# A transformer stack on one core: columns of two input projections reordered, with head norms, index scores and key compression placed between the later panels

## What is computed

```python
def dsa_moba_mixer(h, ...):                                  # block 0, projection "ab_in"
    aq, ak, av, iq, ik, iw, bq, bk, bv = _split(h @ w_in, AB_SIZES)
    aq, ak = partial_rope(rms_norm(aq, ...)), partial_rope(rms_norm(ak, ...))
    iq, ik = partial_rope(iq), partial_rope(ik)              # index heads: no norm
    # score = sum over 8 index heads of iw * relu(iq . ik), causal; the 64 best keys of each query are kept
    o_a = dsa_attention(aq, ak, av, iq, ik, iw)
    bq, bk = partial_rope(rms_norm(bq, ...)), partial_rope(rms_norm(bk, ...))
    o_b = moba_attention(bq, bk, bv)
    return concatenate([o_a, o_b]) @ w_out

def nsa_mixer(h, ...):                                       # block 1, projection "nsa_in"
    q, kc, vc, ks, vs, kw, vw, gt = _split(h @ w_in, C_SIZES)
    q = rms_norm(q, q_norm); q_rot = partial_rope(q)
    kc = rms_norm(nsa_compress(kc, pos_k, w1_k, w2_k), kcmp_norm)   # silu(windows @ w1) @ w2
    vc = nsa_compress(vc, pos_v, w1_v, w2_v)
    ks, kw = partial_rope(rms_norm(ks)), partial_rope(rms_norm(kw))
    gates = sigmoid(gt)
    o = gates . (attention(q, kc, vc), attention(q_rot, ks, vs), attention(q_rot, kw, vw))
    return o @ w_out
```

## Time and profile before

| | us |
|---|---|
| median of 3 runs | 2684.83 |
| the profiled execution's own time | 2688.3 |
| its span | 2686.5 |
| TensorE matmul busy | 2555.4 (95%) |
| VectorE busy | 1120.3 (42%) |
| ScalarE busy | 492.3 (18%) |
| mean granted TensorE clock | 0.959 of full |

### The profile page before, as it was taken

One profiled execution on the slowest core, in us unless ns is written; L12 is line 12 of the kernel. 1 busy time (PEld: TensorE's weight loads), 2 busy tenths in 40 slices (PEclk: granted clock), 3 DMA queues, 4 the chain that ended last, 5 costly groups with the idle time before them and its releaser, 6 DMA issues.

```text
span 2686.5 us, 32881 instructions
## 1 busy us (share of the span) xinstructions
PE 2555.4 (95%) x12508; PEld 2050.3 (76%) x12508; DVE 1120.3 (42%) x2426; ACT 492.3 (18%) x1225; POOL 110.9 (4%) x212
## 2 busy tenths in 40 slices
PE   7789999998898999999999889999999999999997
PEld 4355888846466888588888678889788887689887
DVE  2654212334834023152554445644754553333321
ACT  1132100003512100111210232102123211102210
POOL 0000000000000001000111001110000110000000
PEclk9769999995799999999999999999999999999999
DMA  5113457640023577443777427775326775434441
GB/s 224 65 66 127 150 187 238 226 156 3 1 102 135 181 228 251 147 149 129 256 258 284 147 79 254 258 283 185 117 95 238 258 265 208 166 120 146 150 156 55
DMA packets 122329, 452.98 MB, mean 169 GB/s; under 512 B 13776, under 2 KB 13904, under 8 KB 121680
## 3 DMA queue, kind: packets, MB, share of 16 engines
q1 hardware_dynamic: 92880, 338.24, 35.8%
q0 software_dynamic: 29312, 112.80, 12.2%
HBM read 449.93 MB, written 1.05 MB: 168 GB/s over the span
## 4 chain that ended last, share of the span: by engine, by line
PE 88%; DVE 7%; ACT 2%; issue 1%; DMA 1%; POOL 0%; SPq 0%; DVEq 0%; ACTq 0%
PE pair L460 81%; PE bank L460 6%; DVE att_s L1275 1%; DVE arena L1270 1%; DVE h L1160 1%; ACT arena L941 1%; DVE rstd L1157 1%; PE bank L599 1%; DMA arena<-gmws_dram 1%; ACT arena L953 1%; DVE arena L1678 0%; DVE arena L1674 0%; PE bank L626 0%; DMA cst<-consts_dram 0%; ACT arena L932 0%
## 5 line engine op out<-in xcount | busy, mean ns | idle before, releaser
L460 PE MATMUL pair<-h,ring 128*128 128x256 f32 (+1 forms) x5344 | 1123.6, 373 | 19.6 <-DVE x L1185 6.8
L460 PEld LDWEIGHTS pair<-h,ring 128*128 128x128 f32 x5344 | 989.8, 192 | 149.8 <-DVE x L1185 7.2
L460 PE MATMUL pair<-arena,ring 128*128 128x256 f32 (+1 forms) x3312 | 636.1, 354 | 3.7 <-issue 2.1
L460 PEld LDWEIGHTS pair<-arena,ring 128*128 128x128 f32 x3312 | 567.7, 191 | 72.6 <-issue 3.4
L460 PE MATMUL pair<-ring,h 128*128 128x512 f32 (+1 forms) x768 | 325.5, 584 | 5.5 <-DVE h L1160 3.0
L460 PEld LDWEIGHTS pair<-ring,h 128*128 128x128 f32 x768 | 143.9, 192 | 178.7 <-issue 172.0
L1353 DVE CUSTOM_DVE_ANT_0 adat<-adat,crow,cols 128x1024 f32<-128x1024 f32 x192 | 241.9, 1278 | 8.6 <-DMA adat<-adaw_dram 8.6
L1331 DVE SCALAR_TENSOR_TENSOR arena<-pair,cols,arena 128x255 f32<-128x255 f32 x176 | 84.9, 482 | 279.4 <-ACT arena L989 279.4
L989 ACT ACTIVATE arena<-pair,cols 128x256 f32<-128x256 f32 x176 | 99.2, 564 | 463.3 <-PE pair L460 463.3
L460 PE MATMUL pair<-arena 128*128 128x128 f32 (+7 forms) x946 | 145.0, 359 | 20.6 <-DVE arena L1513 8.6
L911 ACT ACTIVATE h<-x 128x256 f32<-128x256 f32 x84 | 35.0, 417 | 690.4 <-DVE x L1186 364.0
(11 more groups left out here) (197 smaller groups left out, 1310.0 us busy)
## 6 DMA issues: line engine op xcount, KB each, us to landing
ring<-stream_dram SPq DMA_DIRECT2D x638, 512.0 KB, 4.0
adat<-adaw_dram POOLq DMA_DIRECT2D x192, 512.0 KB, 4.6
arena<-gmrows_dram POOLq DMA_DIRECT2D x2, 2560.0 KB, 11.3
arena<-cmpw_dram POOLq DMA_DIRECT2D x1, 2112.0 KB, 8.2
x<-x_in_dram SPq DMA_DIRECT2D x2, 512.0 KB, 4.8
arena<-mem_in_dram SPq DMA_DIRECT2D x1, 1024.0 KB, 12.6
arena<-gmws_dram POOLq DMA_DIRECT2D x2, 512.0 KB, 13.3
out_dram<-h POOLq DMA_DIRECT2D x2, 512.0 KB, 3.8
```

Of the source, the lines that this page charges most:

```text
L460: return nc.tensor.matmul(out, lhsT, rhs, start=start, stop=stop)
```

## The change

The columns of both weight matrices are packed in another order, so that what has most work behind it comes first. For `ab_in`: iq, ik, iw, 88 zero columns, av, k, q, bq, bk, bv. For `nsa_in`: kc, vc, q, ks, kw, vs, vw, gates. The number of tiles stays.

For `ab_in`, in TensorE's program: index transposes behind group 2; index matmuls in four batches of four behind groups 3 to 6, each batch filling two banks with two heads each; the transposes of the other heads in three sets behind groups 5, 7 and 9. ScalarE reads the index banks with ReLU; VectorE's part of the score is then one operation for each head. VectorE's head norms are in three parts (k and q: 9 heads; bq: 8; bk: 8) behind groups 3, 5 and 7, its index rotation behind group 1, and the memory norm moves from group 1 to group 2. For `nsa_in`: transposes of kc and vc behind group 2, the windows behind group 3, compression behind group 4, its output behind group 5, the key norm behind group 6, the transposes of the compressed keys and of q behind group 7, those of the keys behind group 9; the norms of q and the keys in three parts behind groups 3, 5 and 7; the rotation of q behind group 8. The compression writes to banks 5 and 6 instead of 0 and 1. In the diff, TensorE's functions come first, then ScalarE's, then VectorE's with `panels` for `ab_in` and again for `nsa_in`.

```diff
-AB_Q, AB_K, AB_BQ, AB_BK, AB_IQ, AB_IK, AB_AV, AB_BV, AB_IW = 0, 512, 576, 1088, 1600, 1856, 1888, 1952, 2464
-NS_Q, NS_KS, NS_KW, NS_KC, NS_VC, NS_VS, NS_VW, NS_G = 0, 1024, 1280, 1536, 1792, 2048, 2304, 2560
+AB_IQ, AB_IK, AB_IW, AB_AV, AB_K, AB_Q, AB_BQ, AB_BK, AB_BV = 0, 256, 288, 384, 448, 512, 1024, 1536, 2048
+NS_KC, NS_VC, NS_Q, NS_KS, NS_KW, NS_VS, NS_VW, NS_G = 0, 256, 512, 1536, 1792, 2048, 2304, 2560
+AB_PARTS = ((AB_K, 9), (AB_BQ, 8), (AB_BK, 8))
+NS_PARTS = ((NS_Q, 8), (NS_Q + 512, 8), (NS_KS, 8))
...
+                def idx_batch(b):
+                    if b >= 1:
+                        pe.wait_ge(sem("idx_relu"), 2 * b)
+                    for i in range(2):
+                        for a in range(2):
+                            r = 32 * (2 * (b % 2) + a)
+                            last = mm(banks[SB[a]][:, i * TOK:i * TOK + TOK], qrT[r:r + 32, i, b // 2 * P:b // 2 * P + P],
+                                      qrT[r:r + 32, 2, :], True, True)
+                            if i == 1:
+                                last.then_inc(sem("idx_scores"), 1)
+                def ab_between(group):
...
+                    if group == 2:
+                        turns("idx", "idx_rope")
+                    if group == 3:
+                        pe.wait_ge(sem("turn_copied"), turn_sets["idx"][0] + 2)
+                    if 3 <= group < 7:
+                        idx_batch(group - 3)
+                    if group in (5, 7, 9):
+                        turns(f"ab{group // 2 - 2}", "ab_rope", group // 2 - 1)
...
+                def nsa_between(group):
+                    if group == 2:
+                        turns("nsa_c", "freed_dve", FREER[PLAN["nsa_in"].g0 + 1][1])
+                    if group == 4:
+                        compress()
+                    if group == 5:
+                        compress_out()
+                    if group == 7:
+                        pe.wait_ge(sem("kcmp_normed"), 1)
...
+                        turns("nsa_q", "nsa_normed", 2)
+                    if group == 9:
+                        turns("nsa_k", "nsa_rope")
...
                 turn_copies("idx")
-                turn_copies("ab")
+                idx_relu(0)
+                ab_roots(0)
+                idx_relu(1)
+                idx_relu(2)
+                turn_copies("ab0")
+                ab_roots(1)
+                idx_relu(3)
+                turn_copies("ab1")
+                ab_roots(2)
+                turn_copies("ab2")
...
-                roots("nsa_sums", 1, stat[:, 1, 0:TT * 24], P, 1.0 / HD, "nsa_root")
-                act.wait_ge(sem("nsa_gate_in"), 1)
-                nc.scalar.activation(stat[:, 5:7, 0:48], tm[:, :, NS_G:NS_G + 48], ACT.Sigmoid
-                                     ).then_inc(sem("nsa_gates"), 1)
-                turn_copies("nsa_q")
...
                 turn_copies("nsa_c")
-                turn_copies("nsa_k")
+                nsa_roots(0)
                 act.wait_ge(sem("cmp1_done"), 1)
...
                 ins.then_inc(sem("cmp_silu"), 1)
+                nsa_roots(1)
                 roots("kcmp_sums", 1, stat[0:NSA_GROUPS * N_CMP, 2, 0:1], NSA_GROUPS * N_CMP, 1.0 / HD, "kcmp_root")
+                turn_copies("nsa_q")
+                nsa_roots(2)
+                turn_copies("nsa_k")
+                act.wait_ge(sem("nsa_gate_in"), 1)
+                nc.scalar.activation(stat[:, 5:7, 0:48], tm[:, :, NS_G:NS_G + 48], ACT.Sigmoid
+                                     ).then_inc(sem("nsa_gates"), 1)
                 turn_copies("nsa_qr")
...
+                def queries_keys(i):
+                    c0, heads = AB_PARTS[i]
+                    link(heads_normed(i, c0, heads, c0 - AB_K, "ab_sums", "ab_root", i + 1, OT))
+                    rotate(tm[:, :, c0:c0 + heads * HD], heads, HD, 16, 0, view(OT + 1152, 512))
...
+                def index_scores(b):
+                    qt = b // 2
+                    for a in range(2):
+                        dve.wait_ge(sem("idx_relu"), 2 * b + a + 1)
+                        for i in range(2):
+                            hd = 4 * i + 2 * (b % 2) + a
...
+                                ins = V.scalar_tensor_tensor(score[:, qt, :], r, w, score[:, qt, :], ALU.mult, ALU.add)
...
                 def panels(group):
+                    if group == 1:
+                        index_rope()
+                    if group == 2:
+                        memory_norm()
+                    if group == 3:
+                        dve.wait_ge(sem("rows_in"), 16)
+                        queries_keys(0)
+                    if group == 5:
+                        queries_keys(1)
+                        index_scores(0)
+                        index_scores(1)
+                    if group == 7:
+                        queries_keys(2)
+                        V.engine_nop().then_inc(sem("rows_used0"), 1)
+                        index_scores(2)
+                        index_scores(3)
...
                 def panels(group):
+                    if group == 3:
+                        windows()
+                        dve.wait_ge(sem("rows_in"), 16 * 5)
+                        query_parts(0).then_inc(sem("nsa_normed"), 1)
+                    if group == 5:
+                        query_parts(1).then_inc(sem("nsa_normed"), 1)
+                    if group == 6:
+                        compressed()
+                    if group == 7:
+                        link(query_parts(2))
+                        V.engine_nop().then_inc(sem("rows_used2"), 1)
+                        rotated_keys()
+                    if group == 8:
+                        dve.wait_ge(sem("kcmp_turned"), 1)
+                        V.tensor_copy(kcmpT, banks[SB[0]][:, 256:256 + rows]).then_inc(sem("kcmp_done"), 1)
...
+                        rotate(tm[:, :, NS_Q:NS_Q + 1024], NSA_HEADS, HD, 16, 0, view(HID + 4800, 512))
```

## The result

The changed kernel takes **2646.47 us** (median of 4 runs, 2643.95 to 2648.4) against 2686.11 for the kernel before on the same chip (4 runs, 2683.47 to 2687.54): a ratio of 0.9853 [0.9836, 0.987], faster by 39.6 us. Forecast: 2649 (2634 to 2662), 35.9 us gained. The profiled executions span 2643.4 and 2686.5 us.

What follows compares the result with a forecast made beforehand. TensorE, busy 95% of the span, was taken as the bound, with 63 us of gaps behind the two projections to work on. Gains of 21.1 + 13.3 + 1.5 = 35.9 us from a median of 2684.83 gave 2649 us (2634 to 2662).

Steps and rivals of the forecast that it cites:

- ab_in, the sum: From ab_in to the first attention score: score at 104.4 instead of 125.46, 21.1 us gained (19.1 to 21.9).
- Its terms: ab_in's added times: index transposes 0.82 us, four index batches 4.8, head transposes 3.6, last copy to first score 0.7.
- the foreseen wait of 0.62: ab_in's first head transpose set: third job waits 0.6 us for a copy behind two ReLUs on ScalarE.
- nsa_in, the stall and the turns: In nsa_in: 2.58 us stall and 1.9 us of lower clock go; 14 transpose jobs in four sets take 8.8 us.
- The sigmoid of the gates: End of nsa_in: it waits for the last group and adds 0.3 us on ScalarE ahead of the last copies.
- nsa_in, the compression: Behind group 4: clock falls during the step, which takes 10.6 us (6.8 to 13.6); group 5 takes 1.9 us more.
- the forecast's own sign of being wrong: In nsa_in: a compression of 7 or 13.6 us, instead of 10 to 11, would show the forecast wrong.
- Rival 1: In nsa_in: the compression keeps full clock, gaining 5.7 us more, 2643 us in all; chance 0.17.
- Attention 0: First nsa attention: begins at full clock and keeps it for some 3 us, 1.5 us gained.
- Rival 2: nsa attention 0 stays at full clock once it starts there: 11 us, 9.5 beyond those counted, 2639 us; chance 0.12.
- Rivals 3 to 5: Late inserted inputs, 2659 us (0.10); panels lose clock, costing 23 to 110 us (0.02); VectorE's total unchanged, no gain (0.01).
- Total: Whole kernel: 21.1 + 13.3 + 1.5 = 35.9 us gained, giving 2649 us.

Runs made afterwards that it cites:

- e2: Changed kernel with the old ab_in, so only nsa_in has the new column order and inserted work: 2668.67 us, ratio 0.9936 to the kernel before.
- e3: Changed kernel with the 256 compression instructions executed three times in a row behind group 4: 2664.30 us, one execution.
- e4: Changed kernel with the compression issued behind group 3 instead of group 4, so TensorE waits for VectorE's windows directly ahead of it: 2662.07 us, one execution.
- e7: Changed kernel plus four unread matmuls of 256 columns behind the first scores of nsa's attention 0: 2637.47 us, ratio 0.9819 to the kernel before.
- e8: As e7, plus one unread 128-column matmul ahead of each unit's softmax wait in the nsa and DSA attentions: 2633.83 us, ratio 0.9804 to the kernel before.
- e5: Changed kernel with all four index batches of ab_in behind group 9, none between panels: 2652.48 us, one execution.

## Why the prediction was right, and which steps were not

- **ab_in, the sum** (21.1 us): right. The profiled stretch fell by 22.4, but of that 1.6 are the first two groups, 15.58 us before and 14.00 after, which the change does not touch: e2, with the old ab_in, has 14.00 too, e3 and e4, with the new one, 15.53 and 15.61, and e7 17.02, at a clock of 0.50 between 20 and 24 us. From the end of those groups to the first score it is 89.24 us before (125.46 - 36.22) and 68.45 after (101.93 - 33.48): **20.8 us**.
- **Its terms**: index transposes 0.66 to the next panel for 0.82, batches 1.06 each for 1.2, turns 3.9 (1.99, 0.88 and 1.04, with the foreseen wait of 0.62) for 3.6, last copy to score 0.73. One term stood at nothing: a panel beside an inserted step takes 6.96 to 7.07 us for 6.86, 0.7 in all. These four misses nearly cancel. VectorE's part of 8 heads 8.2 us as worked out, 9 heads 9.0 for 9.1, ReLUs 1.08 us a pair. Predicted end 104.4; 101.93 came, and the difference is the start (1.2 us earlier) and the clock of the first groups (1.6), less 0.3.
- **nsa_in, the stall and the turns**: right. No gap over 0.5 us, the groups at full clock. The sigmoid of the gates, foreseen with 0.3 us ahead of the last copies, makes the wait between the last transposes 0.49 us, where the sets before have 0.24.
- **nsa_in, the compression** (10.6 us, and +1.9 for group 5): **this step failed**. It took 7.6 us and group 5 lost nothing (7.06); the forecast's own sign of being wrong was a compression of 7 us. The measured gain of the stretch is 18.4 us for 13.3, and 4.9 of the 5.1 between them are this step. The forecast read the earlier trace rows, a busy TensorE at 0.50 without a rise, as a sign that such work lowers the clock; e3 (22.5 us at 1.00) and e4 (13.8 us at 0.50) show that the compression moves the level neither way. Rival 1 had the mechanism right, 19.0 us for nsa_in; its price of 6.8 us was 0.8 low, since it took 26.5 ns from 11 instructions and all 256 took 29.6 ns each. The section "HAM oscillation — how this bites in real kernels" of TensorE: Matmul & The Clock Gate in the Trainium skill, by which idle gaps lose the clock, had spoken for rival 1. e3, without a gap, and e4, whose window over its gap has 0.80, agree with it; the falls in e7 (at 596) and e8 (at 589), with hardly a wait ahead, are not covered by it.
- **Attention 0** (1.5 us): not there. It takes 35.9 us to the first 256-key row on VectorE before and after; the clock fell within 3 us, behind the waits of its first unit. Rival 2 (full clock once it starts there, 11 us) was wrong for this kernel; in e7 it fails without the first gap too, and in e8, with one filler per unit, the full clock comes. The nsa attentions together are 1.9 us shorter, near the 1.5 by luck: e2, with the same nsa_in, has 119.78 us.
- **Rivals 3 to 5**: no inserted step was late by more than 0.62 us, no panel lost the clock, and both gains stayed.
- **Total**: 35.9 forecast, 39.6 by medians, 43.1 by the profiled spans. The spans have 7.2 more than the forecast: 5.1 in nsa_in, 2.7 in the start and the first groups of ab_in, 0.4 in the nsa attentions, less 0.3 in ab_in's sum and 0.7 elsewhere. Only one execution of each kernel has a profile, so how the 39.6 divides is not settled. The median came within 2.5 us of the 2649 although nsa_in alone was 5.1 off: the kernel before was itself 1.3 us slower in this comparison than the median that the forecast started from (2686.11 for 2684.83), and the medians gained 3.5 us less than the profiled spans. That part of the hit is luck.

## What to carry to other kernels

A serial tail behind a dense projection costs twice: the wait itself, and the lower clock that everything behind the wait runs at. Order the columns so that what needs the long vector work comes out first, cut that work into parts shorter than the slack of the bank copies, and put the light matmul steps between panels where their inputs are surely ready: light work without a gap costs little more than itself there (1.0 us more for four batches, e5), while the compression one group too early costs 13 us (e4). Where a stage can't be kept dense, look at its clock by itself; one matmul in the idle slot of each unit, with four at the start, brought 12 us here (e8).

## What the runs showed of the hardware

- The granted clock kept its level through the gapless compression, whichever it was: the same matmuls of 30 columns ran 22.5 us at 1.00 and 13.8 us at 0.50. "It didn't rise" and "it would fall" are different statements, and a trace of one doesn't show the other.
- Busy share does not tell the level: attention 0 was busy 30.00 of 30.00 us at 0.50 after the change and 24.26 of 26.00 at 1.00 with fillers. At the lower clock the same instructions simply fill the time.
- The clock also fell with hardly a wait ahead: at about 596 in e7, where TensorE had been busy 5.76 of 6.00 us, and at about 589 in e8, inside matmuls of 256 columns. What brings these falls was not found.
- The index matmuls, with 32 input rows and in turn on different rows of the array, took less than the forecast had (1.2): a batch of 8 instructions of 256 columns takes 1.06 us, 132 ns each, where the memory norm's 16 instructions of 256 columns and 128 input rows take 216 ns each (33.31 to 36.77). That the difference is overlap of neighbouring matmuls is argued; no run had them on the same rows.
- The same 32 instructions at the start of ab_in took 14.00 us in five of the ten profiled executions, 15.53 to 15.61 in three and 17.02 in two, not by the version of ab_in. The length goes with the start of the first of them: 14.00 for starts at 18.92 to 19.71 us, 17.02 at 19.94 and 20.01, 15.53 to 15.61 at 20.37 to 20.64.
